# A decoder layer on one core: ScalarE issues all copies of an attention step ahead of both exponentials

## The reference

```python
sc = einsum('bhmqd,bhmkd->bhmqk', qi, k) * scale          # causal, blocks of 128 queries
p  = softmax(where(mask, sc, -inf), axis=-1)
a  = p[:, :, 0] - lam * p[:, :, 1]
out = einsum('bhqk,bhkd->bhqd', a, v)                     # then an RMS norm per head
```

## Time and profile before

| what | value |
| --- | --- |
| median of 3 runs | 2547.55 us (2542.32 to 2547.64) |
| the profiled execution | 2539.64 us, span 2537.9 us |
| PE busy | 2403.2 us, 95% |
| DVE busy | 1560.1 us, 61% |
| ACT busy | 870.7 us, 34% |
| POOL busy | 215.6 us, 8% |
| mean granted clock of PE | 0.973 |

### The profile page before, as it was taken

One profiled execution on the slowest core, in us unless ns is written; L12 is line 12 of the kernel. 1 busy time (PEld: TensorE's weight loads), 2 busy tenths in 40 slices (PEclk: granted clock), 3 DMA queues, 4 the chain that ended last, 5 costly groups with the idle time before them and its releaser, 6 DMA issues.

```text
span 2537.9 us, 30863 instructions
## 1 busy us (share of the span) xinstructions
PE 2403.2 (95%) x11970; PEld 2018.4 (80%) x11970; DVE 1560.1 (61%) x2300; ACT 870.7 (34%) x1371; POOL 215.6 (8%) x145
## 2 busy tenths in 40 slices
PE   6999899967899989899999999999999999999999
PEld 3987888766888878688888888887778888888887
DVE  2648787898989956555454555556655454555554
ACT  2632554158878744221211112123331211112120
POOL 0343044122111000000000000000000000000000
PEclk8999999968999989999999999999999999999999
DMA  6441433120000042211111111115121111111111
GB/s 222 151 153 56 158 121 113 62 67 25 14 9 22 10 149 76 67 50 50 50 46 53 33 51 48 50 63 193 60 67 50 50 38 61 33 50 50 50 50 67
DMA packets 106999, 176.63 MB, mean 70 GB/s; under 512 B 5000, under 2 KB 76956, under 8 KB 105884
## 3 DMA queue, kind: packets, MB, share of 16 engines
q1 hardware_dynamic: 106908, 175.40, 20.8%
HBM read 152.32 MB, written 23.07 MB: 69 GB/s over the span
## 4 chain that ended last, share of the span: by engine, by line
PE 76%; DVE 13%; DMA 4%; ACT 4%; issue 2%; POOL 1%; SPq 0%; ACTq 0%; DVEq 0%; POOLq 0%
PE ps L1755 21%; PE ps L1756 21%; PE ps L1757 21%; DVE ps L1359 2%; PE ps L1936 2%; DVE sb_scores L1563 2%; PE ps L1991 2%; PE ps L1993 2%; PE ps L1921 2%; PE ps L1992 2%; PE ps L1956 2%; DVE sb_w_lo L1270 2%; DVE sb_scores L1579 1%; ACT sb_w_hi L847 1%; DMA sb_w_raw<-in_w_in 1%
## 5 line engine op out<-in xcount | busy, mean ns | idle before, releaser
L1755 PE MATMUL ps<-sb_h_hi,sb_w_hi 128*128 128x512 f32 x1408 | 554.3, 394 | 10.9 <-DVE sb_w_lo L1270 9.1
L1756 PE MATMUL ps<-sb_h_lo,sb_w_hi 128*128 128x512 f32 x1408 | 550.0, 391 | 0.0
L1757 PE MATMUL ps<-sb_h_hi,sb_w_lo 128*128 128x512 f32 x1408 | 549.5, 390 | 0.0
L1705 DVE TENSOR_TENSOR sb_x_new<-sb_x_new,ps 128x512 f32<-128x512 f32 x512 | 344.6, 686 | 212.1 <-PE ps L1757 210.0
L1755 PE MATMUL ps<-sb_w_hi,sb_u_hi 128*128 128x512 f32 x1024 | 399.3, 390 | 9.2 <-DVE sb_x_new L1705 9.2
L1756 PE MATMUL ps<-sb_w_lo,sb_u_hi 128*128 128x512 f32 x1024 | 398.6, 389 | 0.0
L1757 PE MATMUL ps<-sb_w_hi,sb_u_lo 128*128 128x512 f32 x1024 | 398.6, 389 | 0.0
L1197 ACT ACTIVATE sb_relu_t<-ps 128x512 f32<-128x512 f32 x128 | 76.0, 594 | 927.6 <-PE ps L1757 869.7
L1755 PEld LDWEIGHTS ps<-sb_h_hi,sb_w_hi 128*128 128x128 f32 x1408 | 265.5, 189 | 69.6 <-DVE sb_w_lo L1270 10.2
L1756 PEld LDWEIGHTS ps<-sb_h_lo,sb_w_hi 128*128 128x128 f32 x1408 | 265.5, 189 | 56.6 <-issue 1.9
L1757 PEld LDWEIGHTS ps<-sb_h_hi,sb_w_lo 128*128 128x128 f32 x1408 | 265.5, 189 | 55.4
(11 more groups left out here) (201 smaller groups left out, 3115.4 us busy)
## 6 DMA issues: line engine op xcount, KB each, us to landing
sb_w_raw<-in_w_ff SPq DMA_DIRECT2D x64, 1024.0 KB, 5.1
sb_w_raw<-in_w_in SPq DMA_DIRECT2D x18, 1024.0 KB, 5.6
sb_ada<-in_w_ada SPq DMA_DIRECT2D x32, 512.0 KB, 5.9
sb_ada_first<-in_w_ada SPq DMA_DIRECT2D x8, 1024.0 KB, 7.5
sb_x_in<-in_x SPq DMA_DIRECT2D x16, 512.0 KB, 5.1
sb_x_new<-in_x SPq DMA_DIRECT2D x16, 512.0 KB, 4.8
out<-sb_x_new SPq DMA_DIRECT2D x16, 512.0 KB, 4.9
sb_mix_in<-mix_scratch SPq DMA_DIRECT2D x14, 512.0 KB, 4.2
```

The source lines that it names most:

```text
L1705: V.tensor_tensor(out=y, in0=y, in1=psum[:, 4 + o % 4, :], op=ALU.add).then_inc(ff2_read, 1)
L1755: M(dst, ah, bh, start=(n == 0), stop=False)
L1756: M(dst, ah, bl, start=False, stop=False)
L1757: ins = M(dst, al, bh, start=False, stop=(n == last))
```

## The change

ACT's loop issued, in step u: the first exponential of unit u - 1, the first half of the step's copies (rounded up), the second exponential, the other copies. It now issues all copies of the step and then both exponentials. In step 65 the preparation of a weight tile (`wo_head`) keeps its place between the first half of the copies and the rest. Nothing else differs; splits still come at the start of a step, and a root at its end.

```diff
@@ -1117,17 +1117,13 @@
                 if u == LN_STEP + 4:
                     ln_silu(1, 1)
                 items = at_items(u)
-                early = (len(items) + 1) // 2
+                for n, x in enumerate(items):
+                    if u == UNITS + 1 and n == (len(items) + 1) // 2:
+                        wo_head(0, 0, (at_mm, turned(UNITS - 3)))
+                    read_turn(x)
                 if 0 <= u - 1 < UNITS:
                     exp_of(u - 1, 0)
-                for x in items[:early]:
-                    read_turn(x)
-                if 0 <= u - 1 < UNITS:
                     exp_of(u - 1, 1)
-                for n, x in enumerate(items[early:]):
-                    if n == 0 and u == UNITS + 1:
-                        wo_head(0, 0, (at_mm, turned(UNITS - 3)))
-                    read_turn(x)
                 if u == UNITS + 2:
                     wo_head(0, 1, (at_mm, turned(UNITS - 2)))
                 j = att_stage(u, 1)
```

## The result

| | before | after |
| --- | --- | --- |
| median of five runs, same chip | 2547.55 us (2540.12 to 2549.13) | 2559.07 us (2557.3 to 2560.34) |
| ratio, 95% interval | | 1.0053 [1.0039, 1.0068] |
| span of the profiled execution | 2537.9 us | 2557.3 us |
| mean granted clock of PE | 0.973 | 0.967 |

The ratio makes it 13.5 us slower (10 to 17); the forecast was +8, and 2559 is inside its range of 2541 to 2571. The loss is two thirds larger than forecast, and the two traces differ by 19.4 us of span.

What follows compares the result with a forecast made beforehand. It took a ring of DVE's evictions and combine with PE's first half step to bound the attention steps; 8.4 + 2 + 2 - 4.2 = +8.2 us on 2547.55 gave 2555.8, rounded to 2555.5, range 2541 to 2571.

Steps and rivals of the forecast that it cites:

- Step 1: Even steps from 34 on: POOL's split subtraction shuts out combine, 8 steps at 1.05 us, +8.4 us.
- Rival C: Much slower: combine's stalls lower PE's clock in the 8 steps, or a longer ring of copies and exponentials; 2575 us, chance 0.17.
- The early steps, taken as zero: Steps below 34: some overlaps of POOL's split with combine go and some come, net zero.
- Step 4: Steps behind roots: copies no longer wait for table load and exponential; -4.2 us (3.4 at the second root, 0.8 at step 22).
- Steps 2 and 3: Steps of 1024 and 896 columns, +2 us, and the last steps, +2 us: transposes wait for copies now behind exponentials.
- Rival A: POOL never gets ahead of combine, so the splits cost nothing: 2547.3 us, no change, chance 0.27.
- Rival B: Faster: prompt copies remove 10 us of PE's waits for copies and splits cost nothing; 2537.5 us, chance 0.14.

Runs made afterwards that it cites:

- e3: Kernel before, with POOL's split tail made to start when half of the step's evictions are done, as combine is issued: 2573.79 us, ratio 1.0101.
- e1: Changed kernel, with a wait that keeps POOL's split tail until the step's combine has ended: 2531.54 us, ratio 0.9935.
- e11: Changed kernel, with POOL's split tail kept until combine has ended only from step 34 on: 2540.86 us, ratio 0.9992.
- e10: Changed kernel, with POOL's split tail kept until combine has ended only in steps 2 to 33: 2551.19 us, ratio 1.0028.
- e2: Kernel before, with a wait that keeps POOL's split tail until the step's combine has ended: 2537.17 us, ratio 0.9959.
- e7: Kernel of e2, with ACT's new order only in steps 22, 38 and 54, behind the roots: 2531.03 us, ratio 0.9931.
- e5: Kernel of e1, with ACT's old order in steps 63 and 64: 2534.9 us, ratio 0.9952.
- e4: Changed kernel, with ACT's split moved between its copies and its two exponentials from step 2 on: 2545.36 us, ratio 0.9989.
- e9: Kernel of e7, with POOL's two scalings of attention rows each also made to wait until a combine has ended: 2522.09 us, ratio 0.9902.
- e8: Changed kernel, with POOL's split tail kept until combine has ended in step 32 alone: 2556.6 us, ratio 1.0037.

## Why the prediction was right, and where it was not

- **Step 1, the split meets combine: right in kind and nearly in size, but too cheap as a whole.** The 1.05 for a full collision was measured as 1.01 to 1.07 in after (combines 34, 40, 42, 48, 50) and 1.06 of step in e3. Combines 44 and 46 cost 0.66 and 0.54: POOL came 0.23 and 0.35 us ahead of the reciprocal there, not 0.09, and was done earlier. The eight steps that the term counts have 7.3 of excess, and over all late steps it grew by 6.9, against 8.4. As a whole, though, taking the collisions out is worth 30 us in the changed kernel (after against e1) and 10.4 in the one before: the net is +19.7, where the term was +8.4. (One reading of it was off and changed nothing: the L1579 at 712.09 ended 1.34 us behind POOL, not 1.25.)
- **What it left out, the clock.** Rival C had the mechanism, as an alternative with all 8 steps; what happened is the forecast with part of C on top. Behind combine 30, 32 and 48 the clock fell; the steps of combine 30 to 33, 48 and 49 took some 8.5 us more than before beyond their collisions. e11 gives a price to it in the time: the late collisions are worth 15.5 us, for 9.3 of excess that L811 has there. I judged the fall by the length of one wait, 2.24 with and 1.84 without; that the runs show to be no measure (below).
- **The early steps, taken as zero: open.** They had 4.2 us more of excess, and the prediction names one early overlap (642.61) and none of the others. But the 6.4 of e10 isn't a share of the loss: it includes what such collisions cost in the kernel before, whose trace has 4.1 us of early excess beside L811. Ahead of e10 a zero was put at a saving of 7, and the full excess with the fall of the clock at 10; 6.4 with an interval of 5 fits both.
- **Step 4, the roots: right.** -4.2 forecast; 3.2 in the trace at the second root, and 7 with an interval of about 7 between e2 and e7. e7's trace gains 4.1 there. Both traces have a fall of the clock near the third root (13.37 us for one step in e2, 12.32 in e7), so what the third gives isn't told by them.
- **Steps 2 and 3, together +4: not seen in the time.** e1 against e7 is +1. In the trace some of it is there: 0.45 us in the step of combine 28, as predicted; 1.5 and 0.5 in the two steps with layer norm work (14 and 16), which I hadn't priced, and 1.8 back in 17; the steps of combine 56 and 57 (58 and 59 in the prediction's count) were put at a loss and gained 1.8 (7.45 and 8.03 for 8.49 and 8.74). In e7, which has the old order there, PE waited 0.86 us for a copy at 836.14 and at 844.58; in e1, with the new one, there is no such wait in these steps. The tail cost 4 in its own rows and nothing that the time shows (e5), though the time can't tell 4 from nothing.
- **Rival A (POOL never ahead): true in six of the 28 even steps**, those in which L811 took 1.77 to 2.89 us. At 652.18 L1575 came 0.11 us ahead of it, kept its 1.28, and POOL took 2.32. **Rival B** had prompt copies remove 10 us of PE's waits everywhere. With the collisions gone, e1 is 6 faster than e2, and by e7 that stands at the roots.

The two errors had opposite signs: without collisions the order is worth -6 where the sum of steps 2 to 4 was -0.2, with them it costs 19.7 more where 8.4 was put. The net of +13.5 hides both, and a forecast of the net alone would look better than its working was. That the loss came out within 5.5 us of the forecast is in part luck: the undersized term alone would have put it 11 off.

## What to carry to other kernels

Moving one engine's instructions moves what it releases: look where each released instruction of POOL then lands against DVE's work with two SBUF inputs, and if it isn't urgent, tie it with a wait to the end of that work rather than leave its place to chance. In a stage in which PE is nearly always busy, expect a stall to cost more than its length: here 1.3 (e3 against e2) to 1.7 times (after against e1, 30 us for 17.6 of excess), though e4 against after gives 1.0 (16 us for 15.9). A reorder that helps at a few places should be made at those places: three steps of 67 gave all that the times can tell, and together with the two ties it was 1.0% of the whole kernel.

## What the runs showed of the hardware

- **The exclusion was seen in both directions, and with an instruction of one column.** L1573 writes one column and took 1.23 us beside a POOL instruction of 1.28, and 2.02 beside one of 2.37. POOL took 2.32 for 1.28 behind a L1575 that began 0.11 us ahead of it; 0.04 ahead wasn't enough at 660.72. The rows of the 2.32, in after:

```profile
652.18 1.28 DVE L1575 SCALAR_TENSOR_TENSOR sb_scores<-sb_scores,sb_ratio 128x1024 f32<-128x1024 f32 x1
652.29 2.32 POOL L811 TENSOR_TENSOR sb_q_split<-sb_qk_in,sb_q_split 128x512 fp32r<-128x512 f32 x1 [5.96 <-ACT sb_q_split L1054]
```

The Trainium skill, SBUF — State Buffer, section Who interferes with whom, states this contention for a DVE instruction with two SBUF inputs, and that one with at most one SBUF input, as an eviction from PSUM is, doesn't contend. e2 and e9, where POOL works beside evictions, agree: no L811 took over 1.30 us in either, and the excess that is left (5.0 and 1.0) stands beside POOL's work on attention rows.

- **The length of PE's last wait doesn't decide on its clock.** A wait of 1.80 us was followed by 14 us at a mean of 0.51 (e10), one of 1.81, in the same step with the same collision, by none (e8); in after 1.48 was followed by 12 us at 0.72 (794 to 806), before 1.84 by nothing. Behind the same stall e8 lost nothing in the next step and e10 7 us in two, after stretches that were alike in their rows. What the chip goes by in place of the last wait isn't shown by any run here.
